# One recurrent decoder layer on Trainium2: gate tiles in pairs, and the low halves of sixteen weight chunks on GpSimd

## The reference

```python
def rglru_block(h, conv_prev, h_prev, w_in, conv_w, conv_b, w_a, b_a, w_x, b_x, lam, w_out):
    gate_branch, xb = jnp.split(h @ w_in, 2, axis=-1)
    xc, conv_new = causal_conv(xb, conv_prev, conv_w, conv_b)          # 4 taps
    xblk = xc.reshape(B, T, LRU_BLOCKS, LRU_BW)                        # 8 blocks of 128
    r = sigmoid(einsum('btki,kij->btkj', xblk, w_a).reshape(...) + b_a)
    ig = sigmoid(einsum('btki,kij->btkj', xblk, w_x).reshape(...) + b_x)
    log_a = -LRU_C * r * softplus(-lam)
    a = exp(log_a)
    u = sqrt(-expm1(2.0 * log_a)) * (ig * xc)
    u = u.at[:, 0].add(a[:, 0] * h_prev)
    hs = scan of h_t = a_t * h_(t-1) + u_t
    return (hs * gelu(gate_branch)) @ w_out, hs[:, -1], conv_new

def mem_kv(mem, g, w_k, w_v):                                          # once for each layer
    m = rms_norm(mem, g)
    return m @ w_k, m @ w_v
```

## Time and profile before

| | |
|---|---|
| median of 3 runs | 2064.46 us (2064.24 to 2065.48) |
| the profiled execution's own time | 2061.77 us |
| its span, first to last instruction | 2060.1 us |
| mean granted clock of TensorE | 0.949 |
| busy: TensorE / VectorE / ScalarE / GpSimd | 1868.6 / 1473.5 / 1246.7 / 177.9 us |
| high and low halves of the stream's chunks, 212 each: ScalarE / VectorE | 220.5 / 264.3 us |

### The profile page before, as it was taken

One profiled execution on the slowest core, in us unless ns is written; L12 is line 12 of the kernel. 1 busy time (PEld: TensorE's weight loads), 2 busy tenths in 40 slices (PEclk: granted clock), 3 DMA queues, 4 the chain that ended last, 5 costly groups with the idle time before them and its releaser, 6 DMA issues.

```text
span 2060.1 us, 31992 instructions
## 1 busy us (share of the span) xinstructions
PE 1868.6 (91%) x10922; PEld 1608.2 (78%) x10922; DVE 1473.5 (72%) x1769; ACT 1246.7 (61%) x1604; POOL 177.9 (9%) x243
## 2 busy tenths in 40 slices
PE   6978889999889768789769999999999999999994
PEld 6968769999789548688558888888888888888883
DVE  7477436664478455753359888898988889888894
ACT  6555325443367124431268787888878787887873
POOL 2001101000124341010110000000000000000001
PEclk9989899999989889899889999999999999999997
DMA  7544667854434471156469999999999999999993
GB/s 276 193 133 159 243 255 283 352 166 141 160 98 155 170 262 59 46 190 236 184 230 386 370 380 372 380 356 374 378 360 380 374 385 354 372 376 357 393 366 144
DMA packets 151105, 558.74 MB, mean 271 GB/s; under 512 B 16496, under 2 KB 16496, under 8 KB 149568
## 3 DMA queue, kind: packets, MB, share of 16 engines
q1 hardware_dynamic: 139248, 508.58, 67.2%
q0 software_dynamic: 7200, 28.56, 3.7%
q10 hardware_dynamic: 4528, 20.05, 2.4%
HBM read 520.61 MB, written 36.52 MB: 270 GB/s over the span
## 4 chain that ended last, share of the span: by engine, by line
PE 77%; issue 8%; DVE 7%; DMA 4%; ACT 4%; POOL 1%; POOLq 0%; SPq 0%; ACTq 0%; DVEq 0%
PE ps L1663 23%; PE ps L1665 23%; PE ps L1664 23%; DMA raw<-in_stream 2%; DVE w_lo L1059 2%; ACT w_hi L670 2%; PE ps L1949 1%; PE ps L2064 1%; POOL rt L2108 1%; PE ps L1762 1%; PE ps L1793 1%; PE ps L1809 1%; PE ps L1694 1%; DMA y_rows<-ye 0%; PE ps L1784 0%
## 5 line engine op out<-in xcount | busy, mean ns | idle before, releaser
L1564 DVE TENSOR_TENSOR w_lo<-raw,w_hi 128x1024 fp32r<-128x1024 f32 x672 | 787.1, 1221 | 50.6 <-ACT w_hi L989 49.0
L989 ACT ACTIVATE w_hi<-raw 128x1024 fp32r<-128x1024 f32 x672 | 704.6, 1060 | 139.7 <-PE ps L1665 119.9
L1059 DVE TENSOR_TENSOR w_lo<-raw,w_hi 128x1024 fp32r<-128x1024 f32 x212 | 264.3, 1258 | 245.2 <-ACT w_hi L670 243.9
L1663 PE MATMUL ps<-w_hi,xe_hi 128*128 128x512 f32 x896 | 358.2, 400 | 4.7 <-DVE w_lo L1564 4.7
L1665 PE MATMUL ps<-w_hi,xe_lo 128*128 128x512 f32 x896 | 354.5, 396 | 0.0
L1664 PE MATMUL ps<-w_lo,xe_hi 128*128 128x512 f32 x896 | 354.0, 395 | 0.0
L670 ACT ACTIVATE w_hi<-raw 128x1024 fp32r<-128x1024 f32 x212 | 220.5, 1051 | 160.2 <-PE ps L1665 97.2
L1663 PE MATMUL ps<-h_hi,w_hi 128*128 128x288 f32 x928 | 286.1, 308 | 18.4 <-DVE h_lo L1085 14.1
L1664 PE MATMUL ps<-h_lo,w_hi 128*128 128x288 f32 x928 | 280.1, 302 | 0.0
L1665 PE MATMUL ps<-h_hi,w_lo 128*128 128x288 f32 x928 | 278.9, 301 | 0.0
L1663 PEld LDWEIGHTS ps<-h_hi,w_hi 128*128 128x128 f32 x928 | 180.1, 194 | 31.4 <-DVE h_lo L1085 16.8
(11 more groups left out here) (395 smaller groups left out, 2553.1 us busy)
## 6 DMA issues: line engine op xcount, KB each, us to landing
raw<-in_experts SPq DMA_DIRECT2D x672, 512.0 KB, 5.5
raw<-in_stream SPq DMA_DIRECT2D x264, 512.0 KB, 4.4
rest<-in_stream SPq DMA_DIRECT2D x28, 512.0 KB, 5.1
x_rows<-zeros ACTq DMA_DIRECT2D x1, 13824.0 KB, 57.7
out_ssd_s<-s_new POOLq DMA_DIRECT2D x16, 512.0 KB, 4.4
xs<-x_rows POOLq DMA_DIRECT2D x9, 512.0 KB, 4.8
y_rows<-ye POOLq DMA_DIRECT2D x9, 512.0 KB, 7.3
out_k<-kmem ACTq DMA_DIRECT2D x2, 1024.0 KB, 6.6
```

Source lines behind the costliest of these rows:

```text
L989: act.activation(w_hi[:, (NSPLIT + p) % HL, :], raw[:, slot, :], ACT.Copy) \
L1059: dve.tensor_tensor(w_lo[:, o % HL, :], landing_place(k), w_hi[:, o % HL, :].bitcast(F32), ALU.subtract).then_inc(lo_done, 1)
L1564: dve.tensor_tensor(w_lo[:, (NSPLIT + p) % HL, :], raw[:, (NRING + p) % RAW, :], w_hi[:, (NSPLIT + p) % HL, :].bitcast(F32), ALU.subtract) \
L1663: pe.matmul(out, l_hi, r_hi, start=start, stop=False)
```

## The change

It does four things.

1. `PLAN` and the stream: the products `r` and `i` of one tile stand next to each other, ahead of the keys; key tile 0 of the second layer follows tile 2, key tile 1 follows tile 5. TensorE's code has the same order.
2. ScalarE takes the sigmoids in pairs, of tiles 0 and 1 before the last tile's `xc_hi`, of the others behind it. In the convolution it makes the high half for the tile after next before it waits for this tile's `xc`, no longer after it. It makes more high halves in the stage of exp and root, and up to the last key chunk plus the first seven value chunks before `y_lru`.
3. GpSimd makes the low halves of those sixteen chunks (8 of keys, 8 of values) that VectorE made before, under a semaphore of their own: two ahead of its copies of the convolution state, two behind them, one between its eight squares, eleven behind these.
4. The scratch of the first tap moves to another place.

```diff
+KEYS_AFTER = {2: 0, 5: 1}
...
-    p += memory(1)[:EARLY]
-    p += [(("r", j), "act", int(j == 0)) for j in range(KD)]
-    p += [(("i", j), "act", int(j == 0)) for j in range(KD)]
+    for j in range(KD):
+        p += [(("r", j), "act", int(j == 0)), (("i", j), "act", int(j == 0))]
+        if j in KEYS_AFTER:
+            p += memory(1)[KEYS_AFTER[j]:KEYS_AFTER[j] + 1]
...
+POOLED = [PLAN[TAKER[k]][0][:2] in (("k", 1), ("v", 1)) for k in CHUNK_OF]
+NLO = POOLED.count(False)
...
-        conv_t = at("conv_t", [2, PADW], F32, S[8])
+        conv_t = at("conv_t", [2, PADW], F32, S[0])
...
+            for kind in ("r", "i"):
+                if KEY["xb", KD - 1] < g <= KEY[kind, KD - 1]:
+                    cap = min(cap, ORDER[NEED[KEY[kind, 0]] - 1] + HL)
...
+        def halved(o):
+
+            return (lo_pool if POOLED[o] else lo_done), POOLED[:o + 1].count(POOLED[o])
...
             first_tap(0)
+
+            def sigmoids(first, last):
+                for j in range(first, last):
+                    b = ready(("r", j), NT)
+                    act.activation(rg[:, j, :], b, ACT.Sigmoid, bias=par("b_a")[:, j:j + 1]).then_inc(act_freed, 1)
+                    b = ready(("i", j), NT)
+                    act.activation(ig[:, j, :], b, ACT.Sigmoid, bias=par("b_x")[:, j:j + 1]).then_inc(act_freed, 1)
+
             for j in range(KD):
                 if j + 1 < KD:
                     first_tap(j + 1)
+                hi_upto(AHEAD[KEY["xb", min(j + 2, KD - 1)]])
                 act.wait_ge(xc_done, j + 1)
                 act.activation(xc_hi[:, j, :], xc[:, j, :], ACT.Copy).then_inc(xch_done, 1)
-            hi_upto(AHEAD[KEY["k", 1, EARLY - 1]])
+                if j == KD - 2:
+                    sigmoids(0, 2)
+            sigmoids(2, KD)
...
-                hi_upto(AHEAD[KEY["k", 1, max(j, EARLY)]])
+                hi_upto(ORDER[NEED[KEY["k", 1, EARLY]]] + 3 + j)
...
+            hi_upto(ORDER[NEED[KEY["v", 1, 0, 0]] - 3] + HL)
             act.wait_ge(dve_freed, FREED[KEY["k", 1, KD - 1]][1])
             act.dma_start(t["out_k"][1], kmem[1][:, :, :]).then_inc(kv_out, 16)
-            hi_upto(AHEAD[KEY["v", 1, 0, 0]])
...
-                    dve.wait_ge(hi_done, o + 1)
-                    dve.tensor_tensor(w_lo[:, o % HL, :], landing_place(k),
-                                      w_hi[:, o % HL, :].bitcast(F32), ALU.subtract).then_inc(lo_done, 1)
+                    if not POOLED[o]:
+                        dve.wait_ge(hi_done, o + 1)
+                        dve.tensor_tensor(w_lo[:, o % HL, :], landing_place(k),
+                                          w_hi[:, o % HL, :].bitcast(F32), ALU.subtract).then_inc(lo_done, 1)
...
-            keys(1, range(EARLY))
-            for kind in ("r", "i"):
-                k = NEED[KEY[kind, 0]] - 1
-                for j in range(KD):
-                    pe.wait_ge(xcl_done, j + 1)
-                    product((kind, j), [(k, j, j)], xc_hi, xc_lo)
+            for j in range(KD):
+                pe.wait_ge(xcl_done, j + 1)
+                for kind in ("r", "i"):
+                    product((kind, j), [(NEED[KEY[kind, 0]] - 1, j, j)], xc_hi, xc_lo)
+                if j in KEYS_AFTER:
+                    keys(1, [KEYS_AFTER[j]])
             keys(1, range(EARLY, KD))
...
+            def lo_parts(first, last):
+                for o in pooled[first:last]:
+                    pool.wait_ge(hi_done, o + 1)
+                    pool.tensor_tensor(w_lo[:, o % HL, :], landing_place(CHUNK_OF[o]),
+                                       w_hi[:, o % HL, :].bitcast(F32), ALU.subtract).then_inc(lo_pool, 1)
+
+            lo_parts(0, 2)
             pool.wait_ge(dve_freed, FREED[KEY["xb", KD - 1]][1])
...
+            lo_parts(2, 4)
             for k in range(KD):
                 pool.wait_ge(a_done, k + 1)
                 pool.tensor_tensor(expm[:, k, :], decay[:, k, :], decay[:, k, :], ALU.mult).then_inc(sqr_done, 1)
+                if k == 3:
+                    lo_parts(4, 5)
+            lo_parts(5, len(pooled))
```

More of the change, by code:

```diff
@@ L432, in build_program @@
         lo_done = sem("lo_done")
+        lo_pool = sem("lo_pool")
         full = sem("full")
@@ L628, in _ @@
                     if HALVED[before]:
-                        sp.wait_ge(lo_done, ORDER[before] + 1)
+                        sp.wait_ge(*halved(ORDER[before]))
                     else:
@@ L647, in experts @@
                                 .then_inc(s.landed[(NRING + p) % RAW], 16)
-            sp.wait_ge(lo_done, NSPLIT)
+            sp.wait_ge(lo_done, NLO)
             experts(0)
@@ L763, in _ @@
                     first_tap(j + 1)
+                hi_upto(AHEAD[KEY["xb", min(j + 2, KD - 1)]])
                 act.wait_ge(xc_done, j + 1)
                 act.activation(xc_hi[:, j, :], xc[:, j, :], ACT.Copy).then_inc(xch_done, 1)
-            hi_upto(AHEAD[KEY["k", 1, EARLY - 1]])
-            for j in range(KD):
-                b = ready(("r", j), NT)
-                act.activation(rg[:, j, :], b, ACT.Sigmoid, bias=par("b_a")[:, j:j + 1]).then_inc(act_freed, 1)
-            for j in range(KD):
-                b = ready(("i", j), NT)
-                act.activation(ig[:, j, :], b, ACT.Sigmoid, bias=par("b_x")[:, j:j + 1]).then_inc(act_freed, 1)
-            act.wait_ge(c8_done, 1)
-            act.wait_ge(act_freed, FREED[KEY["r", KD - 1]][1])
-            for j in range(KD):
-                hi_upto(AHEAD[KEY["k", 1, max(j, EARLY)]])
+                if j == KD - 2:
+                    sigmoids(0, 2)
+            sigmoids(2, KD)
+            act.wait_ge(c8_done, 1)
+            act.wait_ge(act_freed, FREED[KEY["i", KD - 1]][1])
+            for j in range(KD):
+                hi_upto(ORDER[NEED[KEY["k", 1, EARLY]]] + 3 + j)
                 for k in (2 * (j % 4), 2 * (j % 4) + 1):
@@ L1101, in residual @@
                         lo_upto(NSPLIT)
-                        dve.wait_ge(lo_done, NSPLIT)
+                        dve.wait_ge(lo_done, NLO)
                         dve.engine_nop().then_inc(PASSES[0].lo, RAW)
@@ L1652, in weights @@
                 if o >= used[0]:
-                    pe.wait_ge(lo_done, o + 1)
+                    pe.wait_ge(*halved(o))
                     used[0] = o + 1
@@ L2120, in _ @@
             a.then_inc(cinit, 1)
+            pooled = [o for o in range(NSPLIT) if POOLED[o]]
+            def lo_parts(first, last):
[4 more added lines that the diff above has]
+            lo_parts(0, 2)
             pool.wait_ge(dve_freed, FREED[KEY["xb", KD - 1]][1])
@@ L2370, in stream_inputs @@
     keys_1, values_1 = memory(1)
-    parts += [keys_1[:EARLY]]
     for w in ("lru_w_a", "lru_w_x"):
         parts += [np.asarray(a[w][0]).transpose(1, 0, 2).reshape(1, P, CH)]
-    parts += [keys_1[EARLY:], values_1, columns(a["lru_w_out"][0])]
+    parts += [keys_1, values_1, columns(a["lru_w_out"][0])]
     def attention(l):
```

## The result

The changed kernel takes 2065.81 us, the median of 20 runs (2063.97 to 2070.06); the kernel before, in 20 runs, 2062.77 us (2060.06 to 2067.88). The ratio is 1.0015 with a 95% interval of 1.0008 to 1.0022: **about 3.0 us slower**. That is surely not a gain, and it is smaller than the 0.2% that the prediction took as the least it could tell. The forecast was 2071 us. The profiled execution took 2063.98 us with a span of 2062.4, against 2061.77 and 2060.1 before.

The account below looks back on a forecast made before the run. It took the 105 to 240 us stretch, ending in ScalarE's restart behind `out_v`, as deciding. VectorE's chain ends at 197.3, plus 19.35 gives 216.6 instead of 209.89: 2064.46 + 6.7 = 2071.2 us, range 2052 to 2077.

Parts of the forecast that it names:

- The forecast: Whole kernel: dear GpSimd low halves hold VectorE off, 6.7 us slower, 2071 us, own range 2067 to 2076; chance 0.52.
- the rival of cheap low halves: GpSimd low halves need only a product's 1.90 us and hold VectorE 1.75; -0.3 us, 2064; chance 0.2.
- switch ahead of exp: ScalarE's table switch after the gates: starts at 145.7 us instead of 154.65, 9.0 us earlier.
- first root: ScalarE after exp: at 159.1 us instead of 166.09, with 1.95 us given back by four high halves instead of two.
- from VectorE's first product with a root to the last `xc_hi`: VectorE's chain: 17.0 us without its low halves and key tiles, plus eight GpSimd holds, 18.0 us; 35.0 instead of 21.3.
- from there to the high half behind `out_v`: Behind `y_lru`: 8.05 us for one value chunk, 4.35 to `out_v`'s issue, 6.95 transfer; 19.35 us instead of 20.5.
- The price of a low half: GpSimd's difference of two dense 1024-column tiles: 2.4 us undisturbed, bounds 1.90 and 2.9 us.
- The hold: Each GpSimd low half keeps VectorE's operations with two SBUF inputs waiting 2.25 us.
- side by side: VectorE not held off between the scans, 159 to 178 us; 12.7 us faster, 2052; chance 0.18.
- the convolution: Six tile periods: two save 2.2 us, two beside GpSimd low halves nothing, two 4.5 us; last `xc` 6.7 us earlier.
- rival of a TensorE that stays slow: TensorE at 1.2 GHz through key tile 1, last gates and waits for GpSimd; 3.4 us more, 2075; chance 0.1.
- One for one: Residual: a shift of ScalarE's restart at 209.89 us goes through to the end unchanged, SP at most seven chunks ahead.

Follow-up runs that it names:

- the product with two dense tiles: Changed kernel with GpSimd multiplying instead of subtracting in its sixteen low halves (not true low halves); single run, 2068.22 us.
- the memset: Changed kernel with GpSimd writing zeros by memset in place of the difference in its sixteen low halves; single run, 2049.89 us.
- the last of the six: Kernel before with two lines: convolution high half ahead of the wait for `xc`, no wait for `out_v` before the residual; 2050.9 us, ratio 0.9936.
- the kernel with the order alone: Changed kernel with all low halves back on VectorE, pairs, sigmoids and earlier high halves kept; 2056.64 us, ratio 0.9972 against the kernel before.

## Why the prediction was right in its mechanism and off in a size

**The sign and the mechanism held; the size was 5.4 us too large** (2071.2 worked out, 2065.81 measured). Of that, 3.1 us lie in the instant at which the residual starts (216.6 foretold, 213.51 in the trace) and 1.7 us in the kernel before itself, whose median is 2062.77 over 20 runs instead of 2064.46 over three; 0.6 us is left that no row shows, less than the scatter of the runs.

What came is not what the prediction held likeliest. It gave 0.54 to a loss of over 4.1 us and 0.24 to a time within 4.1 us, and 3.0 us falls in the second. The forecast's own range, 2067 to 2076, missed the time by 1.2 us. The time alone would not have told the forecast from the rival of cheap low halves: counted from 2062.77, +6.7 us gives 2069.5 and -0.3 gives 2062.5, the one 3.7 us too high and the other 3.3 too low. The rows decide between them. And the whole range, 2052 to 2077, holds the unchanged kernel too, so that a time inside it says little.

| instant | foretold | profile | off |
|---|---|---|---|
| low half on GpSimd, undisturbed | 2.4 | 2.36 | |
| end of the last `xc` | about 135 | 132.89 | -2.1 |
| switch ahead of exp | 145.7 | 142.67 | -3.0 |
| first root | 159.1 | 155.99 | -3.1 |
| from VectorE's first product with a root to the last `xc_hi` | 35.0 | 34.2 | -0.8 |
| from there to the high half behind `out_v` | 19.35 | 19.94 | +0.6 |
| high half behind `out_v` | 216.6 | 213.51 | -3.1 |

(The first product is counted from where its turn comes, about 159.4: its row starts at 157.49 and it is held 1.9 us; 162.3 was foretold, so this is 2.9 early. Of the 0.8 us in the next line 0.2 is arithmetic: 21.3 less 3.5 and 1.0 is 16.8, and the prediction wrote 17.0. The last `xc_hi` is counted to 193.57, where the next instruction starts.)

- **The price of a low half** was right: 2.36 us, by the sum's 2.15 ns a column. The rival of cheap low halves fell, and the product with two dense tiles shows why its row was the wrong model.
- **The hold** was right: products from 0.43 to 2.59 us and scans from 0.69 to 2.78 are 2.1 to 2.2 us of hold, 2.25 were foretold. Eight low halves stand in the chain, as counted: from 159.4 to 180.76 are 8.1 periods of 2.64 us. The rival "side by side" needed scans at 0.69 us; its 2052 us is close to what the memset gave (2049.89), the one case in which they do run side by side, but with operations of 0.95 us, so the closeness is in part chance.
- **The step that was mis-sized is the convolution.** The prediction put GpSimd's two low halves on two tiles, each "4.83 us, nothing gained". Both ran in a row, and nearly all of their hold fell on the taps of one tile:

```profile
117.74 4.81 DVE L1150 SCALAR_TENSOR_TENSOR conv_t<-conv,small,conv_t 128x312 f32<-128x312 f32 x2
```

  The two taps take 4.81 us where they take 1.11 alone: 3.7 us of hold for the two low halves, where 4.5 were counted; part of the first ran beside the scalings of `xb` (from 117.31), which are not held. That tile took 6.22 us (`xc` from 116.78 to 123.00) and the other 2.51, 8.7 together instead of 9.7. The two tiles that keep the low half took 3.32 and 3.66 instead of 3.74, and the first `xc` came 0.6 us earlier. In all the last `xc` is 8.8 us earlier than before, not 6.7. A smaller part, 0.9 us, came up to the switch: TensorE was at its upper level in the ninth gate product, where the prediction had it at the lower for five products.

```profile
126.61 0.58 PE L1682 MATMUL ps<-mem_hi,w_hi 128*128 128x256 f32 x1 [1.85 <-DVE conv L1203]
...
134.09 0.40 PE L1682 MATMUL ps<-xc_hi,w_hi 128*128 128x288 f32 x1 [1.36 <-ACT rg L778]
134.32 0.30 PE L1683 MATMUL ps<-xc_lo,w_hi 128*128 128x288 f32 x1
```

  It had worked without a gap from 126.61 to 132.7, key tile 0 and three matmuls of the gates, at a granted clock of 0.50 up to 132 us, 0.77 between 132 and 133, and 1.00 from there on; the gap of 1.36 us ahead of the ninth product did not bring the clock down. That undoes the first half of the rival of a TensorE that stays slow. It was at the lower level again, 0.50, from 195 to 200 us, behind its wait for GpSimd's last low half; the sum had that in the 4.65 us taken from a cold start.
- **Where the gain went.** The order gives 5.9 us, all of it by one line in the convolution. The early switch and the early roots that the pairs bring end at VectorE, which is not ready for them: with its own low halves it is behind, with GpSimd's it is held. A rival that the prediction lacked is this one, that part of the change has no effect at all.
- **One for one.** The shift of the high half behind `out_v` against the shift of the medians: +3.6 and +3.0 (the change), -5.6 and -5.9, -5.9 and -6.2, +8.6 and +8.6, -12.4 and -12.4, -12.4 and -11.2. That step held in six kernels to 1.2 us, by their medians. Single executions scatter more: the profiled one of the change was 2.2 us over that of the kernel before where the instant is 3.6 later, and that of the last of the six 8.8 under it where the instant is 12.4 earlier. The instant tells two kernels apart better than one run's time.

## What to carry to other kernels

GpSimd is no free hand for VectorE: beside each operation tried here in which it reads SBUF (difference, product, copy) VectorE's operations with two SBUF inputs stood still for nearly its whole length. So moving work of 1.2 us on VectorE to 2.4 us on GpSimd loses where VectorE is on the path and its next operations read two SBUF tiles; beside VectorE's idle time or its reads of PSUM, or where GpSimd merely writes, it is not held. Before reordering what comes early in a stretch, find the engine that ends it; here one line (a ready piece of work ahead of a wait in the same engine's queue) gave all that a whole new order gave. And look at the end of the stretch for waits that guard more than the next writer needs: the one for `out_v` was worth about 7 us here, and two value chunks moved into idle time 5.5 more.

## What the runs showed of the hardware

- GpSimd, 1024 float32 columns, undisturbed: difference of two dense tiles 2.36 us, product of two dense tiles 2.35, copy 1.04, memset 0.95; the product with a broadcast input has 1.90. The dense tiles read go with the price, and difference or product makes none; the type written was not varied.
- A scan on VectorE is held like a product: 2.78 us instead of 0.69. When both engines have work queued, they take turns: in the changed kernel nine products and scans in a row are each held once, by one low half. Key tiles, with one input in PSUM, stay at 0.39 us.
- GpSimd is held the other way too: its last two small copies of the state, `lru_new_h`, took 1.20 and 1.29 us beside VectorE's low halves (1.2 us each) in the changed kernel, and 0.49 and 0.52 beside its `y_lru` products (0.45 us each) in the kernel with the order alone; in the kernel with the memset the first of them, not held, took 0.20.
- The transfer of `out_v`, always the same size, held the next high half for 6.87 us in one kernel and 9.44 in another. What sets that was not tried.
